# Compression inputs of the attention computed once and their halves swapped on TensorE, compression weights in eight pieces, one input split moved

## The reference, cut to what matters

```
kv = (rmsnorm(h, kv_norm) @ w_kv).reshape(bsz, s, N_BRANCH, 2, N_KV_GROUPS, HEAD_DIM)   # 3 branches, k and v, 4 groups, 64
k_c = rmsnorm(compress(kv[:, :, 0, 0], pe_k, w1_k, w2_k), k_norm[0])
v_c = compress(kv[:, :, 0, 1], pe_v, w1_v, w2_v)
# branches 1 and 2 give k_s, v_s, k_w, v_w; keys are normalised

def compress(raw, pe, w1, w2):
    idx = arange(nc)[:, None] * 16 + arange(32)[None, :]        # nc = 15 blocks of 32 tokens, 16 apart
    blk = raw[:, idx] + pe                                      # per group: 15 blocks x (32 * 64)
    return gelu(blk @ w1) @ w2                                  # w1: 2048 x 128, w2: 128 x 64

h = h + 0.5 * swiglu_ffn(rmsnorm(h, ffn1_norm[i]), ffn1_w_in[i], ffn1_w_out[i])         # the gated stage behind it
```

## Time and profile before

| | us |
|---|---|
| median of 3 executions | 1631.26 (1631.18 to 1633.62) |
| the profiled execution | 1631.32 |
| its span, first to last instruction | 1629.4 |
| TensorE busy | 1589.8 |
| VectorE busy | 1083.8 |
| ScalarE busy | 866.3 |

### The profile page before, as it was taken

The page is one execution under the profiler, slowest core; times in us unless marked ns, Lnnn a source line. Parts: engine busy times, 40 slices in busy tenths (PEclk is TensorE's granted clock), DMA queues, the critical chain, the costliest instruction groups (busy, mean ns, idle before and its releaser), DMA issues.

```text
span 1629.4 us, 33428 instructions
## 1 busy us (share of the span) xinstructions
PE 1589.8 (98%) x11692; PEld 1497.6 (92%) x11692; DVE 1083.8 (67%) x1822; ACT 866.3 (53%) x1380; POOL 151.3 (9%) x133
## 2 busy tenths in 40 slices
PE   7899999999999999999999999998999999999999
PEld 7789998977999889999999999888999888999997
DVE  6768766635777566666787766767576655686665
ACT  5676554444666445545445545544565546665443
POOL 1650000165100000000000000000000023200000
PEclk9999999989999999999999999999999999999999
DMA  6126556543565656566565566666456872065554
GB/s 233 65 66 206 183 183 189 176 153 124 163 204 188 191 183 194 184 189 195 185 203 187 190 190 185 198 200 196 144 193 193 231 197 77 2 194 185 188 194 142
DMA packets 81247, 282.83 MB, mean 174 GB/s; under 512 B 8848, under 2 KB 12432, under 8 KB 81168
## 3 DMA queue, kind: packets, MB, share of 16 engines
q1 hardware_dynamic: 77376, 276.88, 53.3%
q10 hardware_dynamic: 3792, 4.85, 1.5%
HBM read 280.12 MB, written 1.57 MB: 173 GB/s over the span
## 4 chain that ended last, share of the span: by engine, by line
PE 92%; DVE 4%; ACT 2%; issue 1%; ACTq 1%; DMA 0%; DVEq 0%; SPq 0%
PE psum L1654 18%; PE psum L1655 17%; PE psum L1656 17%; PE psum L1646 17%; PE psum L1647 9%; PE psum L1782 2%; PE psum L1784 2%; PE psum L1783 2%; PE psum L2049 1%; PE psum L2000 1%; DVE w_lo L980 1%; PE psum L1948 1%; PE psum L2033 0%; DVE w1c_all L1532 0%; PE psum L1853 0%
## 5 line engine op out<-in xcount | busy, mean ns | idle before, releaser
L535 ACT ACTIVATE w_hi<-raw 128x1024 fp32r<-128x1024 f32 x522 | 550.9, 1057 | 453.9 <-PE psum L1656 263.5
L980 DVE TENSOR_TENSOR w_lo<-raw,w_hi 128x1024 fp32r<-128x1024 f32 x476 | 581.8, 1223 | 230.1 <-ACT w_hi L535 229.4
L1654 PE MATMUL psum<-xs,w_hi 128*128 128x256 f32 x1960 | 549.4, 280 | 5.7 <-DVE w_lo L980 4.9
L1656 PE MATMUL psum<-xs,w_lo 128*128 128x256 f32 x1960 | 547.9, 280 | 0.0
L1655 PE MATMUL psum<-xs,w_hi 128*128 128x256 f32 x1960 | 547.8, 279 | 0.0
L1646 PE MATMUL psum<-hs,w_hi 128*128 128x512 f32 x1216 | 421.9, 390 | 0.0
L1654 PEld LDWEIGHTS psum<-xs,w_hi 128*128 128x128 f32 x1960 | 368.9, 188 | 6.8 <-DVE w_lo L980 5.4
L1655 PEld LDWEIGHTS psum<-xs,w_hi 128*128 128x128 f32 x1960 | 369.0, 188 | 0.2
L1656 PEld LDWEIGHTS psum<-xs,w_lo 128*128 128x128 f32 x1960 | 369.1, 188 | 0.0
L1647 PE MATMUL psum<-hs,w_lo 128*128 128x256 f32 x1216 | 342.9, 282 | 0.0
L1646 PEld LDWEIGHTS psum<-hs,w_hi 128*128 128x128 f32 x1216 | 228.3, 188 | 47.7
(11 more groups left out here) (280 smaller groups left out, 1558.8 us busy)
## 6 DMA issues: line engine op xcount, KB each, us to landing
raw<-tiles SPq DMA_DIRECT2D x522, 512.0 KB, 4.2
bias<-bias_dram ACTq DMA_DIRECT2D x8, 256.0 KB, 6.5
x<-x_in SPq DMA_DIRECT2D x4, 256.0 KB, 5.3
y_out<-x SPq DMA_DIRECT2D x8, 128.0 KB, 3.3
con<-consts SPq DMA_DIRECT2D x1, 771.0 KB, 8.9
bias_dram<-bias_row ACTq DMA_DIRECT2D x1, 512.0 KB, 7.2
row<-rows SPq DMA_DIRECT2D x1, 192.0 KB, 8.8
vec<-vecs SPq DMA_DIRECT2D x1, 80.5 KB, 2.1
```

The source lines that it names most:

```text
L535: act.activation(w_hi[s][:, :], raw[s][:, :], ACT.Copy).then_inc(hi_ready, 1)
L980: dve.tensor_tensor(w_lo[s][:, :], raw[s][:, :], hi_of(w_hi[s][:, :]), ALU.subtract).then_inc(lo_ready, 1)
L1654: pe.matmul(out, w_hi[s][:, c:c + P], x_hi, start=first, stop=False)
L1656: return pe.matmul(out, w_lo[s][:, c:c + P], x_hi, start=False, stop=last)
```

## The change

- `kvc` has 4 tiles and not 8: each result holds two groups of 64 features once. VectorE scales it whole into a new buffer `c_flat`, then writes both halves that stand right already: upper rows to the one group, lower rows, shifted by one token, to the other.
- TensorE multiplies each `c_flat` with a permutation `c_turned_rows` that swaps the two halves of the rows (`swap_rows`, fp32, into banks 6 and 7 in turn). ScalarE copies the swapped halves to their places (`other_rows`). `swap_rows` 0 to 2 stand behind tiles 1 to 3 of `kvc`, number 3 behind tile 2 of `glu_2`. ScalarE does `other_rows` 0 and 1 at the end of `nsa_kv`, 2 behind tile 0 and 3 behind tile 2 of `glu_2`.
- TensorE's `keys_turned` waits for all four swapped pairs as well (`c_swapped`), and moves from tile 3 to 4.
- The first weights of the compression are laid out by rows on the host and loaded in eight pieces of 256 KB (runs of 2 KB), one behind each of the tiles 0 to 7 of `glu_2`; the two transfers of `w2c` follow behind tile 8. `compress` waits for ten transfers, and moves from tile 8 to 10; its followers move by two tiles too.
- The input split of `glu_2` moves into stage `kv`: one `split_x` on ScalarE behind each split, one `rest_x` on VectorE behind each take_lo.

```diff
-    ("kv", 8, 4), ("kvc", 8, 8), ("glu_2", 44, 44), ("out_2", 24, 8),
+    ("kv", 8, 4), ("kvc", 4, 4), ("glu_2", 44, 44), ("out_2", 24, 8),
...
+        c_flat = [part(c_at - 1024 + S * o, S) for o in range(4)]
+        c_turned_rows = part(c_at - 1024 - P, P)
...
             def nsa_kv():
                 root("kvn")
-                used("kv", 8)
                 for k in range(KD):
+                    used("kv", k + 1, k)
                     split_x(hi_part(os_, k), x[:, k * S:(k + 1) * S], vec[:, VEC["pre_1"] + k:VEC["pre_1"] + k + 1])
...
-                used("kvc", 8)
-
-                for j, w in enumerate((w1c_k, w1c_v)):
-                    act.dma_start(w1c[j].rearrange("p (c n) -> p c n", n=P), w.rearrange("(c p) n -> p c n", p=P)).then_inc(c_loaded, 16)
+                for o in range(4):
+                    used("kvc", o + 1, o)
+                    if o >= 2:
+                        other_rows(o - 2)
+
+            def other_rows(o):
+
+                act.wait_ge(c_swap, o + 1)
+                dup, g = c_dup[o // 2], 2 * (o % 2)
+                act.activation(dup[0:DH, (g + 1) * S:(g + 2) * S], bank(6 + o % 2, 0, S, slice(0, DH)), ACT.Copy)
+                act.activation(dup[DH:P, g * S:(g + 1) * S - 1], bank(6 + o % 2, 1, S, slice(DH, P)), ACT.Copy).then_inc(c_swapped, 1)
+
+            def compression_weights(n):
+
+                j, c = divmod(4 * n, CBLOCK // 2)
+                act.dma_start(w1c[j][:, c * P:(c + 4) * P], (w1c_k, w1c_v)[j][:, c * P:(c + 4) * P]).then_inc(c_loaded, 16)
+
+            def compression_outputs():
+
                 act.dma_start(w2c[0], w2c_k).then_inc(c_loaded, 16)
                 act.dma_start(w2c[1], w2c_v).then_inc(c_loaded, 16)
 
+            def early(u):
+                if u == 0:
+                    other_rows(2)
+                    key_roots()
+                if u == 2:
+                    other_rows(3)
+                compression_weights(u)
...
-            glu("glu_2", {0: key_roots, 9: compressed_hidden, 11: compressed_squares, 13: compressed_roots})
+            glu("glu_2", {u: lambda u=u: early(u) for u in range(8)} |
+                {8: compression_outputs, 11: compressed_hidden, 13: compressed_squares, 15: compressed_roots})
...
             def nsa_kv():
+
+                def pre(k):
+                    g = VEC["pre_1"] + k
+                    rest_x(lo_part(os_, k), x[:, k * S:(k + 1) * S], vec[:, g:g + 1], hi_part(os_, k), XS0["pre_1"] + k + 1)
...
-                            lambda o: 4 * (1 + o // 2))
-                rest_all("pre_1", os_)
+                            lambda o: 4 * (1 + o // 2), each=pre)
+                then(dve.memset(c_turned_rows, 0.0))
+                for e in range(2):
+                    ins = dve.tensor_copy(c_turned_rows[:, e * DH:(e + 1) * DH], ident[:, (1 - e) * DH:(2 - e) * DH])
+                then(ins)
...
-                for o in range(8):
+                for o in range(4):
                     b = (OUT0["kvc"] + o) % 4
-                    dst = c_dup[o // G][:, (o % G) * S:(o % G + 1) * S]
+                    dup, g = c_dup[o // 2], 2 * (o % 2)
                     dve.wait_ge(tile_done, TILE0["kvc"] + o + 1)
-                    dve.tensor_tensor(dst[0:DH, :], bank(b, 0, S, slice(0, DH)), rb[0:DH, :], ALU.mult)
-                    dve.tensor_tensor(dst[DH:P, 0:S - 1], bank(b, 1, S, slice(DH, P)), rb[DH:P, 1:S], ALU.mult).then_inc(out_read, 1)
+                    dve.tensor_tensor(c_flat[o], bank(b, 0, S), rb[:, :], ALU.mult).then_inc(c_flat_, 1)
                     take_lo(TILE0["kvc"] + o + RING)
+                    dve.tensor_tensor(dup[0:DH, g * S:(g + 1) * S], bank(b, 0, S, slice(0, DH)), rb[0:DH, :], ALU.mult)
+                    dve.tensor_tensor(dup[DH:P, (g + 1) * S:(g + 2) * S - 1], bank(b, 1, S, slice(DH, P)), rb[DH:P, 1:S], ALU.mult)\
+                       .then_inc(out_read, 1)
...
-            glu("glu_2", {0: keys, 4: keys_turned, 9: compression_bias, 15: compressed})
+            glu("glu_2", {0: keys, 4: keys_turned, 11: compression_bias, 17: compressed})
...
-                feature("kvc", 8, "kvn")
+                feature("kvc", 4, "kvn", between={u: lambda u=u: swap_rows(u - 1) for u in range(1, 4)})
+
+            def swap_rows(o):
+
+                pe.wait_ge(c_flat_, o + 1)
+                if o >= 2:
+                    pe.wait_ge(c_swapped, o - 1)
+                pe.matmul(bank(6 + o % 2, 0, S), c_turned_rows, c_flat[o], start=True, stop=True).then_inc(c_swap, 1)
...
                 pe.wait_ge(c_kn, 1)
+                pe.wait_ge(c_swapped, 4)
...
-                pe.wait_ge(c_loaded, 16 * 4)
-                pe.wait_ge(out_read, OUT0["kvc"] + 8)
+                pe.wait_ge(c_loaded, 16 * 10)
+                pe.wait_ge(out_read, OUT0["kvc"] + 4)
...
-            feature("glu_2", 2 * FF2, "pre_1", os_, between={3: keys_turned, 8: compress, 11: compressed, 13: compressed_sums})
+            feature("glu_2", 2 * FF2, "pre_1", os_, between={2: lambda: swap_rows(3), 4: keys_turned, 10: compress, 13: compressed, 15: compressed_sums})
...
+def by_rows(w):
+
+    return np.ascontiguousarray(w.reshape(-1, P, w.shape[1]).transpose(1, 0, 2).reshape(P, -1))
...
-        feature_tiles(np.stack([kv[:, 0], kv[:, 0]], axis=3).reshape(D, -1)), glu[2], out[2],
+        feature_tiles(kv[:, 0].reshape(D, -1)), glu[2], out[2],
```

More of the change, by code:

```diff
@@ L233, in build @@
             sem(f"c_{n}") for n in ("loaded", "sqd", "sum", "std", "bias", "gelu", "kc", "kcsqd", "kcss", "kcstdd"))
+        c_flat_, c_swap, c_swapped = (sem(f"c_{n}") for n in ("flat", "swap", "swapped"))
         c_kn, c_kt, c_kT, c_hd, c_vcd, c_end = (sem(f"c_{n}") for n in ("kn", "kt", "kT", "hd", "vcd", "end"))
@@ L1022, in narrow, with token_major @@
                 dve.tensor_copy(fsum[b][0:width, :], bank(b, 0, S, slice(0, width))).then_inc(out_read, 1)
-            def token_major(name, outs, dst, tiles_, col=0):
+            def token_major(name, outs, dst, tiles_, col=0, each=lambda t: None):
                 for o in range(outs):
@@ L1029, in token_major @@
                         take_lo(TILE0[name] + t + RING)
+                        each(t)
                     dve.wait_ge(tile_done, TILE0[name] + tiles_(o))
@@ L1036, in token_major @@
                         take_lo(TILE0[name] + tiles_(o) - 1 + RING)
+                        each(tiles_(o) - 1)
             def residual_one(name):
@@ L2221 @@
         "x_in": np.ascontiguousarray(a["x"][0].T.reshape(KD, P, S).transpose(1, 0, 2).reshape(P, KD * S)), "tiles": tiles, "vecs": vecs, "rows": rows, "consts": constants(),
-        "rel_bias": np.ascontiguousarray(a["rel_bias_2"][:, heads]), "w1c_k": a["cmp_w1_k_2"], "w1c_v": a["cmp_w1_v_2"],
+        "rel_bias": np.ascontiguousarray(a["rel_bias_2"][:, heads]), "w1c_k": by_rows(a["cmp_w1_k_2"]), "w1c_v": by_rows(a["cmp_w1_v_2"]),
         "w2c_k": w2[0], "w2c_v": w2[1],
```

## The result

The changed kernel takes 1618.9 us (median of four executions, 1615.17 to 1625.26), the kernel before on the same chip 1632.4 (four, 1631.18 to 1633.97): ratio 0.9919, interval 0.9892 to 0.9946. The forecast was 1614.2 with a range of 1611.5 to 1618.5, so the time lies 0.4 us above the range. It is faster, as foretold, by 13.5 us (0.8%) and not by 17.1.

A forecast was written before the change was run, and what follows sets the result against it. TensorE, busy 98% of the span, was taken as the bound; -11.2 + 0.8 + 1.7 - 7.7 + 1.4 - 2.1 = -17.1 us, so 1631.3 became 1614.2 us, range 1611.5 to 1618.5.

The forecast's parts named there:

- Tiles removed: Stage kvc: four of eight tiles go, at 2.80 us each; -11.2 us.
- first c_flat: Behind kvc tile 1: TensorE waits for VectorE's first scaled result; +0.8 us idle, bounds 0 and 2.
- permutation: In kvc and glu_2: four fp32 products on TensorE at 0.43 us each, without waits; +1.7 us.
- Input split at no cost: Stage kv: splits and rests moved between its tiles cost nothing; without this cover, at most 3.25 us.
- The hole and the new wait: Ahead of keys_turned: TensorE's old wait goes, -7.7 us; a wait for c_swapped 4 comes, +1.4, bounds 0 and 3.
- Clock: Behind the old hole in glu_2: the 2.4 GHz level stays, giving back 2.1 us.
- Rival (a): At the new hole: the clock falls and about 2.1 us return; 1616.3 to 1617.3 us, chance 0.17.
- Eight pieces: glu_2: issues near 0.3 us each, hidden in ScalarE's 1.4 us free per tile.
- Rival (d): glu_2: each piece holds ScalarE 4.05 us, as the second old transfer did; 1636 us, chance 0.02.
- rival (c): Compression waits for weights: a tile or the last weights land 2 to 4 us late; 1616.2 to 1618.2, chance 0.10.
- The last small weights: Ahead of the compression: landing 3.8 us after issue, TensorE coming 5.6 us after tile 8; no cost, bounds 0 to 2.
- So the same time serves both: Starting time of the sum: profiled execution 1631.3 us and median of three runs 1631.26 taken as one.

The follow-up runs named there:

- split_back: Changed kernel with the input split of glu_2 put back behind stage kv, as in the kernel before; 1623.43 us, ratio 0.9938.
- before_pieces: Kernel before with only the weights changed: eight pieces behind tiles 0 to 7 of glu_2, small ones behind tile 8; 1624.36 us, ratio 0.9945.
- after_whole: Changed kernel with the old two large weight transfers and the two small ones at the end of nsa_kv; 1623.9 us, ratio 0.9949.
- rows_early: Changed kernel with the last pair of half copies behind tile 1 of glu_2, not tile 2; 1623.83 us, ratio 0.9918.
- before_warm: Kernel before with more filler products on TensorE early in the program, nothing of the change; 1632.27 us, ratio 0.9991.
- rows_w2c: Changed kernel with the last half copies behind tile 1 of glu_2 and the small weights behind tile 5; 1614.81 us, ratio 0.9882.

## Why the prediction was right or wrong

The direction and the mechanism were right, the time was 4.7 us too low. Two steps made it so: the time to which the sum was added, and the size of the hole, both read from one execution.

- *What bounds the kernel*: right. The wins were TensorE's own work, its hole and its clock; in the stretch no other part of the edit is seen to move the time.
- *Tiles removed*, *first c_flat*, *permutation*: right. The first product of glu_2 comes 13.08 us after the first of kvc (1103.36 to 1116.44); the forecast had 13.3. The idle piece ahead of the first permutation is 0.51 where I put 0.8, between bounds of 0 and 2.
- *Input split at no cost*: right, 23.10 us of kv before and 23.07 after; split_back took the cover away, with 3.28 us of idle time and a low clock behind it.
- *The hole and the new wait*: the cause was right. 7.53 us are gone, 1.31 stand in their place, released by ScalarE's copy as named and not by the keys. before_pieces and after_whole show the cause from both sides. The size, **-7.7**, was a **mis-sized term**: it is that of one execution, and the holes of the two other profiles of this code are 1.1 and 2.0 us shorter. One slip of reading did no harm: the split that starts at 1132.39 is that of the fifth tile of glu_2, since ScalarE had split tiles 0 to 3 during kvc, the first at 1112.91.
- *Clock*: right in glu_2, which has 1.00 throughout. Rival (a) at the new holes didn't come. The row that spoke for it was misread: ahead of 1327.95 stand two idle pieces, 0.81 and 0.86 us, with 1.5 us between their ends.
- *Eight pieces*: the issues are as forecast, 0.33 to 0.42 us. Rival (d) needed 3.5 us an issue and is out. The 270 GB/s of rival (c) should have been 278 (786,432 bytes in 2.83 us); the profile has 287.
- *The last small weights*: "landed 3.8 us after issue ... Nothing, with 0 to 2 as bounds" was a **mis-sized term**. I took one landing for all. They landed between 3.7 and 8.0 us after issue, TensorE waited 1.17 us in one execution of the changed kernel and not at all in another, and in rows_early 3.22. At that end the clock comes in as well, which my bounds left out: 5.3 us more for the compression. By the forecast's own signs the 1.17 us are rival (c), in small.
- *"So the same time serves both"*: this is **the step that failed**. It set the sum of one profiled execution against the median of three and took their agreement for the centre. The four executions beside the result have 1632.4, and the kernel before has its centre at 1634.2 over 44. From the 1634.2 the forecast of -17.1 gives 1617.1, 1.8 us under what was measured, so the step accounts for 2.9 of the 4.7 us; by the four alone it is 1.1. The rest, 1.8 to 3.6, is the sum.

In the stretch, which takes the early scatter out, three profiles of the kernel before (163.24, 162.59 and 160.80) stand against three of the changed one (147.94, 146.77 and, with fillers, 146.49). The edit brings 12.9 to 16.8 us by them, 15.1 between the means. So the sum of 17.1 was about 2 us too large. The hole accounts for 1.0 of that (the mean of the three holes is 6.5, against 7.53), the wait for the small weights for 0.4 (1.17 us in one of three). The remainder is smaller than what one execution differs from the next.

The range failed for a plain reason: it was made from the bounds of the edit's terms and held none of the spread of an unchanged kernel, which is 11.7 us over 44 executions. The statement that a measurement tells 0.2%, 3.3 us, from no change stood in the text, and the range didn't use it.

Open is the late landing of tiles in out_2 of the first changed profile. It cost 1.9 us of idle time, with a granted clock of 0.50 in the 4 us behind it; the rest of the 4.6 stands beside clocks like that. It was seen in one of 14 profiles, and its cause wasn't tried. But a loss in this part doesn't need the edit. From the first tile of out_2 to the first of glu_3 ten of the 14 profiles take 178.2 to 179.8 us and four 182.8 to 184.3: the changed kernel's first, split_back, rows_early, and before_warm, which has nothing of the edit. In before_warm TensorE's idle pieces there are the same as in before (2.2, 0.9, 0.8 and 0.3 us), and only the clock differs. Two times the same 4 us of work, in before and then in before_warm:

```profile
1358.10:1362.10 4.00, 4.00 (x34) 3.67 (x33) 3.04 (x16) 3.23 (x12) 0.00 (x0) 1.00 0.10 39
```

```profile
1354.20:1358.20 4.00, 4.00 (x21) 3.64 (x20) 2.98 (x16) 3.23 (x11) 0.00 (x0) 0.61 0.13 51
```

So I count the loss to the execution and not to the edit; for the late tiles that is argued and not shown.

## What to carry to other kernels

A transfer can cost the engine that issues it, not only the DMA, above all when it is issued right behind a large one: look at the issue's own duration on the queue, and at what stands behind it on that engine. When a wait is removed, price the next one at its worst landing and with the clock behind it, and leave slack for the last small transfer, which is cheap to issue early. A forecast from one profiled execution should carry that kernel's own scatter, in its centre and in its range.

## What the runs showed of the hardware

- **Issue time by shape and place.** 1 MB in 2048 pieces of 512 bytes took the queue 0.85 to 0.89 us for the first transfer and 2.25 to 4.05 for the second, and 4.69 to 4.99 for the 64 KB behind them (four profiles); the same 64 KB took 0.33 in the changed kernel, 2.8 us behind a piece of 256 KB. 256 KB in 128 runs of 2 KB took 0.33 to 0.42. Whether size, runs or spacing does it wasn't separated.
- **Landing of a small transfer.** The last 64 KB took 3.7 to 5.9 us from issue to landing in 13 profiles and 8.0 in rows_early. The stretch ahead of the compression moves 287 GB/s in the changed kernel's first profile. The Trainium skill (DMA: Bandwidth & Descriptors, Latency and other measured facts) gives 0.2 us on average and 2 us at high load for an access to the chip's memory; by an estimate from these two figures, 1.8 us, load covers less than half of the 4.3 us between the ends here. Of the Trainium skill's rule to issue early and wait late (DMA: Bandwidth & Descriptors, Rules for kernel authors) the profiles bear out that TensorE doesn't wait when the small weights go out behind tile 5 (no idle piece in rows_w2c, 3.22 us in rows_early).
- **Clock behind an idle piece.** After 3.22 us without work the compression ran at 0.50 to 0.54 of the clock over the 17 us that follow, though TensorE was busy throughout, 17.30 of 17.50 us. After 3.28 us in split_back it was 0.57 for 4 us. After 1.17 and 1.31 us the stretches behind have 1.00, and after 1.84 us the compression took the same 8.60 us. An idle piece isn't needed for a fall: in the two rows above on out_2 to glu_3 the same work ran at 1.00 and at 0.61, TensorE being busy by the profile 4.00 of 4.00 us in both, and without an idle piece in the 8 us ahead in before_warm.
- **Scatter by the clock.** From run to run the span follows the mean granted clock: the kernel before 1627.1 at 0.991 and 1638.9 at 0.983, the changed one 1613.3 at 0.992 and 1623.4 at 0.986. The product of span and clock has about half the spread of the span (standard deviation 1.6 against 2.9 us for the kernel before, 1.3 against 3.0 for the changed one), though the clock is known to a thousandth only, which is 1.6 us. In the twelve executions of before_warm it has no smaller spread than the span (2.7 against 2.6). The means of the product are 1610.5 and 1599.3. By an estimate from them about 11 us of the edit's gain would remain at equal clock and the rest be clock that it gives back; no run measures that.
